# First attention heads: the seventh row block's weights are formed before the eighth's maxima, and a modulation sum moves from the sixth to the fourth row block

## The chip, the cores and the metric

The kernel runs on one core of a Trainium2 chip. The metric is the device time of one execution in microseconds (us). TensorE (PE in the profile, PEld for its weight loads) multiplies, VectorE (DVE) and ScalarE (ACT) do the elementwise work, GpSimd (POOL) splits weights, and SyncE (SP) issues the DMAs.

## What is computed

Two layers of a decoder trunk on x (1024 tokens by 1024 features, float32). Layer 0 has 4 differential attention heads beside 8 dilated sliding-window heads, layer 1 has gated linear attention; each is followed by a SwiGLU feed-forward, and norms and gates are modulated by silu(c) @ ada_w. The change lies in the differential heads:

```python
s = jnp.einsum('bhcqd,bhckd->bhcqk', qb, kf)          # c = 0, 1: two score maps of a head
s = jnp.where(causal, s - slope * dist, -jnp.inf)
p = jax.nn.softmax(s, axis=-1)
w = p[:, :, 0] - lam * p[:, :, 1]                      # the weights of a row block
o = jnp.einsum('bhqk,bhkv->bhqv', w, vf)               # row blocks of 128 queries
mod = jax.nn.silu(c) @ ada_w[l] + ada_b[l]             # the modulation
```

## The kernel before

Each engine has a program of its own, written out by hand; semaphores tie them together, and each engine works strictly in its written order. The heads of layer 0 run as eight blocks b = 0 to 7. Blocks 0 to 3 (kind 0) are the differential heads, one each; 4 to 7 (kind 1) hold two dilated heads each. Within a block, n = 0 to 7 are row blocks of 128 queries; row block n looks at K = 128 (n + 1) keys. In the text row blocks and heads are counted from one: the seventh row block is n = 6.

A row block of kind 0 goes round the engines like this:
- TensorE forms the two score maps (`scores(n)`, L981), two row blocks ahead.
- VectorE, in `biased(b, n)`, adds the bias, takes the row maxima of both maps while writing them from PSUM to `pr[n % 2]` (L2176, two instructions), and negates the maxima (L2181).
- ScalarE exponentiates both maps in place and sums the rows (`exps(n)`, L1572).
- VectorE takes the reciprocals (L2210), forms the coefficient lam * r1 / r0 (L2213, 128x1), and adds the second map times it to the first (L2217). These are the weights; the semaphore `w_done` goes up.
- TensorE waits for `w_done` and transposes the weights (`turn_weights(n)`, L1002) into PSUM banks 4 and 5; ScalarE (L1566) and VectorE (`copies(n)`, L2191) copy them to SBUF, and TensorE multiplies them by the values (`weigh(n)`, L1015), one row block later.

Between these TensorE has other work: for n = 0 to 4 a chunk of the next block's input projection (`chunk`, L824 to L828), for n = 5 to 7 a third of its last chunk (`filler(0)` to `filler(2)`, L846 to L852). Its order for a row block of kind 0 is chunk or filler, `scores(n + 2)`, `turn_weights(n)`, `weigh(n - 1)`. `scores(n)` waits until VectorE has read the maps of row block n - 1. `biased(b, n)` waits for the scores and until the transposes of row block n - 2 have read `pr[n % 2]`.

ScalarE goes through `copies(n - 1)`, `output(n - 2)`, `exps(n + 1)`. After `exps(4)` and `exps(6)` it rounds a streamed weight unit (`hi_u`, L1378), and GpSimd then forms that unit's low part (L702, `w_lo` from `w_raw` and `w_hi`).

VectorE also sums the modulation: `ada_step(e)` (L2139 to L2150) adds one of eight slices of ada_w, scaled by silu(c), to an accumulator (L2143 for the first, L2145 for the others: 128x1024, all operands in SBUF), and then drains. A head has eight such sums, numbered 0 to 7 here, one in each row block before the change. The slices stream through two buffers. SP asks for slice e once sum e - 2 is done, in the order: weight unit, slices 2 to 5, weight unit, slices 6 and 7, weight unit, slices 8 and 9; a weight unit waits for GpSimd to be done with the one two before.

Of the kernel before, what the change touches and what calls it, by code (L numbers as in the profile page):

```python
# [51 lines left out]
def trunk_kernel(nc, xT, cT, weights, ada_w, ada_bT, norm_gT, lam_p, subln_g, w_g2, b_g2, head_g,  # L52
# [5 lines left out]
    with ctx:  # L58
# [47 lines left out]
        def bank(b, n=512):  # L106
            return ps[:, b * 512:b * 512 + n]
# [272 lines left out]
        def lane_count(kind, n, lane):  # L380

            return 1 + sum(g[1] == lane for m in range(n) for g in lanes(kind, m))

        def events(b, t):
            return LANE[0] * min(b, 4) + LANE[1] * max(b - 4, 0) + t
# [1483 lines left out]
        def _(v):  # L1869
# [267 lines left out]
            def ada_step(e):  # L2137

                v.wait_ge(ada_full[e % 2], 16 * (e // 2) + 16)  # L2139
                if e % 8 == 0:  # L2140
                    if e:
                        v.wait_ge(ada_mm, e // 8 + 1)
                    v.tensor_scalar(acc_one, ada_two[:, e % 2, :], cs[:, 0:1], None, ALU.mult).then_inc(ada_used, 1)  # L2143
                else:
                    v.scalar_tensor_tensor(acc_one, ada_two[:, e % 2, :], cs[:, e % 8:e % 8 + 1], acc_one, ALU.mult, ALU.add)\  # L2145
                        .then_inc(ada_used, 1)
                if e % 8 == 7:
                    v.drain().then_inc(acc_done, 1)
                else:
                    v.drain()  # L2150

            def attention():
                def biases(kind):

                    for c in range(kind + 1):
                        v.scalar_tensor_tensor(bias[:, c, :], dist, slope[:, c:c + 1], mask_bias, ALU.mult, ALU.add)
                    v.drain()

                def copy_v(b, group):
                    v.wait_ge(pv_done, 8 * b + 1)  # L2160
                    v.wait_ge(td_done, group)
                    v.tensor_copy(v_tok[:, 4:8, :], bank(5).rearrange("p (m q) -> p m q", q=P)).then_inc(td_free, 1)

                def biased(b, n):

                    kind = b // 4
                    for c in range(2):
                        K = P * (n + 1)
                        col = 2 * n + c
                        v.wait_ge(s_done[c], 8 * b + n + 1)  # L2170

                        if n > 1:
                            v.wait_ge(ta_done, events(b, lane_count(kind, n - 1, 0)))
                            v.wait_ge(td_done, events(b, lane_count(kind, n - 1, 1)))
                        v.sem_inc(waited, 1)
                        v.tensor_tensor_reduce(out=pr[n % 2][:, c, 0:K], in0=ps[:, c * 1024:c * 1024 + K],  # L2176
                                               in1=bias[:, c if kind else 0, 1024 - K:1024], scale=SCORE_SCALE,
                                               scalar=-3.0e38, op0=ALU.add, op1=ALU.max,
                                               accum_out=mx[:, col:col + 1]).then_inc(s_read[c], 1)
                    v.drain()  # L2180
                    v.tensor_scalar(nmx[:, 2 * n:2 * n + 2], mx[:, 2 * n:2 * n + 2], -1.0, None, ALU.mult).then_inc(nm_done, 1)  # L2181

                def block_(kind, b, last=False):
                    before = lambda t: events(b, t)
                    count = 1

                    def copy_d(dst, m):
                        nonlocal count
                        count += 1
                        v.wait_ge(td_done, before(count))  # L2190
                        v.tensor_copy(dst, bank(5)[:, 0:m * P].rearrange("p (m q) -> p m q", q=P)).then_inc(td_free, 1)  # L2191

                    def copies(n):
                        for c, lane, k0, m in lanes(kind, n):
                            if lane == 1:
                                if n > 1:
                                    v.wait_ge(pv_done, 8 * b + n)
                                copy_d(wT[n % 2][c][:, k0:k0 + m, :], m)

                    for n in range(8):  # L2200
                        a0 = 2 * n
                        if n and kind == 1:
                            copies(n - 1)
                        if n < 7:
                            biased(b, n + 1)
                        if n and kind == 0:
                            copies(n - 1)
                        v.wait_ge(exp_done, 16 * b + 2 * n + 2 + 1)
                        if kind == 0:
                            v.reciprocal(r0[:, a0:a0 + 2], rs[:, a0:a0 + 2])  # L2210
                            v.drain()

                            v.scalar_tensor_tensor(coef, r0[:, a0 + 1:a0 + 2], neglam, rs[:, a0:a0 + 1], ALU.mult, ALU.mult)  # L2213
                            v.drain()
                            K = P * (n + 1)
                            p = pr[n % 2]
                            v.scalar_tensor_tensor(p[:, 0, 0:K], p[:, 1, 0:K], coef, p[:, 0, 0:K], ALU.mult, ALU.add)\  # L2217
                                .then_inc(w_done, 1)
                        else:
                            v.reciprocal(r0[:, a0:a0 + 2], rs[:, a0:a0 + 2]).then_inc(w_done, 1)  # L2220
                        if n < 4 and not last:
                            evict(6 * (b + 1) + n)
                        if n == 1 and b:
                            columns(b, b + 1, 1)
                        if b < 7:
                            ada_step(8 * b + n)
                    copies(7)

                    if b == 3:
                        v.wait_ge(tab_full, 48)  # L2230
                        v.memset(slope[:, 0:1], 0.5)
                        v.memset(slope[:, 1:2], 0.25)
                    else:
                        v.tensor_scalar(slope, slope, 0.25, None, ALU.mult)
                    v.drain()
                    if not last:
                        biases((b + 1) // 4)
                        biased(b + 1, 0)
                    if kind == 0:
                        v.wait_ge(sub_root, b + 1)  # L2240
                        v.reciprocal(ms, ms)
                        v.drain()
                        v.tensor_scalar(ms, ms, 1.0 - LAM_INIT, None, ALU.mult)
                        v.drain()
                        v.tensor_tensor(o_sb, o_sb, ms.rearrange("p (n u) -> p n u", u=1).broadcast_to([P, 8, P]), ALU.mult)
                    if kind == 0:
                        v.drain().then_inc(o_ready, 1)
                    if not last:
                        copy_v(b + 1, before(LANE[kind]))
                    for half in range(2):  # L2250
                        v.wait_ge(y_hi, 2 * b + half + 1)
                        high, lower = ((hh[half][:, b, :], hl[half][:, b, :]) if last else
                                       (t[:, half * HALF:(half + 1) * HALF] for t in (y_st_hi, y_st_lo)))
                        if kind == 0:
                            v.scalar_tensor_tensor(lower, bank(4 + half), sub_g, high.bitcast(f32), ALU.mult, ALU.subtract)\
                                .then_inc((ta_free, td_free)[half], 1)
                        else:
                            v.tensor_tensor(lower, bank(4 + half), high.bitcast(f32), ALU.subtract)\
                                .then_inc((ta_free, td_free)[half], 1)
                    v.drain().then_inc(blk_done, 1)  # L2260

                v.wait_ge(tab_full, 32)
                v.memset(slope, 0.25)
                v.drain()
                biases(0)
                copy_v(0, 1)
                biased(0, 0)
                for b in range(HEADS):
                    block_(b // 4, b, b == HEADS - 1)
# [275 lines left out]
```

## Time and profile before

| | us |
|---|---|
| median of three runs | 2646.45 |
| lowest and highest | 2639.69, 2649.98 |
| the profiled execution | 2640.05 |
| its span | 2638.1 |
| TensorE busy | 2517.8 (95%) |
| VectorE busy | 1368.4 (52%) |
| GpSimd busy | 1144.6 (43%) |
| ScalarE busy | 1075.4 (41%) |

The profile is of one execution. In its timeline a line is: start, length, engine, line of the kernel, operation, what is written and read, shapes, and, in brackets, how long the engine had been idle and what released it. The granted clock of TensorE is given as a share of 2.4 GHz, so 0.5 is 1.2 GHz. The four differential heads lie between 95 and 352 us, some 65 us each.

### The profile page before, as it was taken

The numbers are of one execution on the slowest core, as the hardware profiler recorded it, in microseconds if no ns is written. First come the engines' busy times: TensorE is split into PE (matmuls) and PEld (weight loads), VectorE is DVE, ScalarE is ACT, GpSimd is POOL, SyncE is SP. The second block draws the span as 40 slices with busy tenths as digits, with TensorE's granted clock in tenths as the row PEclk, the third lists the DMA queues.
The fourth block names the chain that finished last, engine by engine and source line by source line (L and its number), as shares of the span: only waits on it lengthen the run. The fifth ranks groups of instructions, "written<-read, shape, count | busy, mean of one in ns | idle before, by whom it ended". The sixth has DMA issues, their size and how long they took to land.

```text
span 2638.1 us, 33909 instructions
## 1 busy us (share of the span) xinstructions
PE 2517.8 (95%) x12152; PEld 2058.3 (78%) x12152; DVE 1368.4 (52%) x1877; ACT 1075.4 (41%) x1837; POOL 1144.6 (43%) x648
## 2 busy tenths in 40 slices
PE   5999999999999999999999999998999999999996
PEld 3777778878788888888887777887778888888885
DVE  6566665551574333554356446668556332455145
ACT  3354454344553333334333236555545233334222
POOL 0111111013557777444444434443666777544443
PEclk8999999999999999999999999999999999999998
DMA  6233332234242222442534842213333221343343
GB/s 267 64 104 104 113 112 81 101 116 174 88 128 88 80 71 73 159 135 96 168 111 169 286 136 73 71 67 109 96 100 108 89 88 65 120 143 112 112 136 110
DMA packets 106886, 305.14 MB, mean 116 GB/s; under 512 B 11456, under 2 KB 11776, under 8 KB 106752
## 3 DMA queue, kind: packets, MB, share of 16 engines
q1 hardware_dynamic: 106752, 303.40, 34.1%
q8 instruction: 79, 1.29, 0.2%
q14 instruction: 55, 0.45, 0.1%
HBM read 262.46 MB, written 40.89 MB: 115 GB/s over the span
## 4 chain that ended last, share of the span: by engine, by line
PE 60%; issue 17%; POOL 7%; DVE 7%; DVEq 3%; ACT 3%; POOLq 2%; DMA 1%; SPq 0%; ACTq 0%
PE ps L828 7%; PE ps L824 7%; PE ps L825 7%; PE ps L1277 5%; PE ps L1274 5%; PE ps L1273 5%; POOL w_lo L702 5%; PE ps L1015 3%; PE ps L1304 3%; PE ps L1307 3%; PE ps L1301 3%; PE ps L1105 2%; PE ps L1002 2%; DVEq L2316 2%; PE ps L981 1%
## 5 line engine op out<-in xcount | busy, mean ns | idle before, releaser
L702 POOL TENSOR_TENSOR w_lo<-w_raw,w_hi 128x1024 fp32r<-128x1024 f32 x258 | 629.0, 2441 | 1300.5 <-ACT w_hi L1372 595.9
L824 PE MATMUL ps<-h_hi,w_hi 128*128 128x512 f32 x1200 | 479.3, 399 | 20.8 <-DVE h_lo L1918 9.3
L825 PE MATMUL ps<-h_lo,w_hi 128*128 128x512 f32 x1200 | 469.4, 391 | 0.0
L1372 ACT ACTIVATE w_hi<-w_raw 128x1024 fp32r<-128x1024 f32 x178 | 188.3, 1058 | 436.5 <-PE ps L1307 286.5
L1986 DVE TENSOR_TENSOR a_lo<-arena,a_hi 128x512 fp32r<-128x512 f32 x88 | 205.5, 2336 | 207.7 <-ACT a_hi L1843 207.7
L828 PE MATMUL ps<-h_hi,w_lo 128*128 128x512 f32 x1200 | 298.2, 391 | 0.0
L824 PEld LDWEIGHTS ps<-h_hi,w_hi 128*128 128x128 f32 x1200 | 226.0, 188 | 84.9 <-DVE h_lo L1918 15.6
L828 PEld LDWEIGHTS ps<-h_hi,w_lo 128*128 128x128 f32 x1200 | 226.6, 189 | 47.4
L825 PEld LDWEIGHTS ps<-h_lo,w_hi 128*128 128x128 f32 x1200 | 226.3, 189 | 47.4 <-issue 2.4
L1273 PE MATMUL ps<-comb,w_hi 128*128 128x512 f32 x560 | 217.8, 389 | 0.0
L1274 PE MATMUL ps<-comb,w_hi 128*128 128x512 f32 x560 | 217.8, 389 | 0.0
L751 POOL TENSOR_TENSOR w_lo<-a_f,w_hi 128x512 fp32r<-128x512 f32 x112 | 144.6, 1293 | 79.0 <-ACT w_hi L1466 79.0
L1301 PE MATMUL ps<-a_hi,w_hi 128*128 128x512 f32 x672 | 167.0, 390 | 0.9 <-DVE ybuf L2044 0.9
L1304 PE MATMUL ps<-a_lo,w_hi 128*128 128x512 f32 x672 | 166.0, 389 | 0.0
L1307 PE MATMUL ps<-a_hi,w_lo 128*128 128x512 f32 x672 | 165.9, 389 | 0.0
L1466 ACT ACTIVATE w_hi<-a_f 128x512 fp32r<-128x512 f32 x112 | 70.8, 632 | 230.3 <-PE ps L1277 83.2
L1572 ACT ACTIVATE pr_flat<-pr_flat,small 128x256 f32<-128x256 f32 (+7 forms) x128 | 98.3, 770 | 134.3 <-DVE small L2181 134.2
L1277 PE MATMUL ps<-comb,w_lo 128*128 128x512 f32 x560 | 149.7, 389 | 0.0
L1301 PEld LDWEIGHTS ps<-a_hi,w_hi 128*128 128x128 f32 x672 | 126.0, 188 | 28.5 <-DVE ybuf L2044 1.7
L1307 PEld LDWEIGHTS ps<-a_hi,w_lo 128*128 128x128 f32 x672 | 126.2, 188 | 26.2
L1304 PEld LDWEIGHTS ps<-a_lo,w_hi 128*128 128x128 f32 x672 | 126.2, 188 | 26.2
L1274 PEld LDWEIGHTS ps<-comb,w_hi 128*128 128x128 f32 x560 | 105.1, 188 | 21.8
(269 smaller groups left out, 4374.5 us busy)
## 6 DMA issues: line engine op xcount, KB each, us to landing
w_raw<-weights SPq DMA_DIRECT2D x286, 512.0 KB, 3.6
arena<-ada_w SPq DMA_DIRECT2D x80, 512.0 KB, 3.5
arena<-act_d SPq DMA_DIRECT2D x72, 256.0 KB, 3.8
act_d<-ybuf SPq DMA_DIRECT2D x56, 256.0 KB, 2.2
arena<-ada_w SPq DMA_DIRECT2D x8, 1024.0 KB, 15.1
x<-xT SPq DMA_DIRECT2D x4, 2048.0 KB, 10.9
glr<-weights SPq DMA_DIRECT2D x14, 512.0 KB, 3.6
rinv<-weights SPq DMA_DIRECT2D x28, 256.0 KB, 4.1
```

The source lines that it names most:

```text
L702: pool.tensor_tensor(w_lo[:, s, :], w_raw[:, s, :], w_hi[:, s, :].bitcast(f32), ALU.subtract).then_inc(lo_done, 1)
L824: pe.matmul(bank(b), w, high[:, k, :], start=k == 0, stop=False)
L825: pe.matmul(bank(b), w, low[:, k, :], start=False, stop=False)
L828: mm = pe.matmul(bank(b), w_lo[:, s, k * P:(k + 1) * P], high[:, k, :], start=False, stop=k == KB - 1)
L1273: pe.matmul(bank(b), w, high[:, k, :], start=k == 0, stop=False)
L1274: pe.matmul(bank(b), w, low[:, k, :], start=False, stop=False)
L1277: mm = pe.matmul(bank(b), combo_part(w_lo, q)[:, k * P:(k + 1) * P], high[:, k, :], start=False, stop=k == KB // 2 - 1)
L1301: pe.matmul(bank(m), w_hi[:, slot, cols[m]], a_hi[:, s, :], start=first, stop=False)
L1304: pe.matmul(bank(m), w_hi[:, slot, cols[m]], a_lo[:, s, :], start=False, stop=False)
L1307: mm = pe.matmul(bank(m), w_lo[:, slot, cols[m]], a_hi[:, s, :], start=False, stop=False)
L1372: a.activation(w_hi[:, slot, :], w_raw[:, slot, :], ACT.Copy).then_inc(hi_done, 1)
L1986: v.tensor_tensor(a_lo[:, u % 2, :], act_source(half, u), a_hi[:, u % 2, :].bitcast(f32), ALU.subtract)\
```

## The change

In blocks of kind 0 two things are moved in VectorE's program; no instruction is added or taken away, and no other engine's program is touched.

- `biased(b, 7)`, which stood ahead of the seventh row block's copies and weights, stands behind its weights (L2217).
- The sums are spread otherwise: row blocks n = 0 to 7 do sums 0; 1; 2; 3 and 4; 5; none; 6; 7. Before, row block n did sum n.

Blocks of kind 1 keep their order.

```diff
-                        if n < 7:
+                        if n < 6 or n == 6 and kind:
                             biased(b, n + 1)
                         if n and kind == 0:
                             copies(n - 1)
...
                             v.scalar_tensor_tensor(p[:, 0, 0:K], p[:, 1, 0:K], coef, p[:, 0, 0:K], ALU.mult, ALU.add)\
                                 .then_inc(w_done, 1)
+                            if n == 6:
+                                biased(b, 7)
...
                         if b < 7:
-                            ada_step(8 * b + n)
+                            first, end = ((0, 1), (1, 2), (2, 3), (3, 5), (5, 6), (6, 6), (6, 7), (7, 8))[n] if kind == 0 else (n, n + 1)
+                            for e in range(first, end):
+                                ada_step(8 * b + e)
```

## Rows read from the trace of the kernel before

**Rows 1.** The page's own lines: span, TensorE's share, and the sums' DMA issues.
```profile
span 2638.1 us, 33909 instructions
...
PE 2517.8 (95%) x12152; PEld 2058.3 (78%) x12152; DVE 1368.4 (52%) x1877; ACT 1075.4 (41%) x1837; POOL 1144.6 (43%) x648
...
arena<-ada_w SPq DMA_DIRECT2D x80, 512.0 KB, 3.5
```

**Rows 2.** The waits, 90 to 345 us: waiter, releaser, total us, times, longest.
```profile
PE ps L1002 <- DVE pr_flat L2217: 9.7, 6, 2.3
```

**Rows 3.** Timeline (start, length, engine, line), second head, fifth row block's stretch.
```profile
193.06 0.33 SPq L484 DMA_DIRECT2D arena<-ada_w  x1
193.37 0.96 DVE L2176 CUSTOM_DVE_ANT_0 pr_flat<-ps,arena 128x768 f32<-128x768 f32 x1 [0.34 <-issue]
196.54 0.88 DVE L2217 SCALAR_TENSOR_TENSOR pr_flat<-pr_flat,small 128x640 f32<-128x640 f32 x1
197.34 1.28 DVE L2145 SCALAR_TENSOR_TENSOR rinv<-arena,cs,rinv 128x1024 f32<-128x1024 f32 x1
198.56 0.53 PEld L1002 LDWEIGHTS ps<-ident,pr_flat 128*128 128x128 f32 x5 [0.26 <-issue]
199.61 1.09 DVE L2176 CUSTOM_DVE_ANT_0 pr_flat<-ps,arena 128x896 f32<-128x896 f32 x1 [0.99 <-PE ps L1002]
```

**Rows 4.** Timeline, two neighbouring sums of the later input projection (x2 is both).
```profile
1523.28 2.66 DVE L2077 SCALAR_TENSOR_TENSOR arena<-arena,cs 128x1024 f32<-128x1024 f32 x2
```

**Rows 5.** Timeline, second head: the seventh block's maxima, its exponentials, GpSimd's instruction.
```profile
201.82 0.17 DVE L2181 TENSOR_SCALAR small<-small 128x2 f32<-128x2 f32 x1
202.02 1.04 ACT L1572 ACTIVATE pr_flat<-pr_flat,small 128x896 f32<-128x896 f32 x1 [1.05 <-DVE small L2181]
202.65 1.02 DVE L2217 SCALAR_TENSOR_TENSOR pr_flat<-pr_flat,small 128x768 f32<-128x768 f32 x1
203.73 0.87 PE L1002 MATMUL ps<-ident,pr_flat 128*128 128x128 f32 x6
205.21 2.40 POOL L702 TENSOR_TENSOR w_lo<-w_raw,w_hi 128x1024 fp32r<-128x1024 f32 x1 [13.26 <-ACT w_hi L1378]
205.21 1.23 DVE L2176 CUSTOM_DVE_ANT_0 pr_flat<-ps,arena 128x1024 f32<-128x1024 f32 x1 [0.34 <-issue]
```

**Rows 6.** Timeline, second head: from the eighth maxima to the eighth transposition.
```profile
207.68 0.17 DVE L2181 TENSOR_SCALAR small<-small 128x2 f32<-128x2 f32 x1
207.78 0.42 DVE L2191 COPY wt_flat<-ps 128x256 f32<-128x256 f32 x1
207.88 1.15 ACT L1572 ACTIVATE pr_flat<-pr_flat,small 128x1024 f32<-128x1024 f32 x1 [1.41 <-DVE small L2181]
208.65 1.15 DVE L2217 SCALAR_TENSOR_TENSOR pr_flat<-pr_flat,small 128x896 f32<-128x896 f32 x1
209.03 1.13 ACT L1572 ACTIVATE pr_flat<-pr_flat,small 128x1024 f32<-128x1024 f32 x1
209.86 1.75 PE L1002 MATMUL ps<-ident,pr_flat 128*128 128x128 f32 x7 [2.29 <-DVE pr_flat L2217]
212.19 0.16 DVE L2210 RECIPROCAL small<-small 128x2 f32<-128x2 f32 x1
212.71 1.28 DVE L2217 SCALAR_TENSOR_TENSOR pr_flat<-pr_flat,small 128x1024 f32<-128x1024 f32 x1
215.47 1.04 PE L1002 MATMUL ps<-ident,pr_flat 128*128 128x128 f32 x8
```

**Rows 7.** Timeline, second head, fourth row block: GpSimd beside a modulation sum.
```profile
189.58 2.37 POOL L702 TENSOR_TENSOR w_lo<-w_raw,w_hi 128x1024 fp32r<-128x1024 f32 x1 [31.66 <-ACT w_hi L1378]
190.62 2.41 DVE L2145 SCALAR_TENSOR_TENSOR rinv<-arena,cs,rinv 128x1024 f32<-128x1024 f32 x1
```

**Rows 8.** Windows, second and fourth head: length, engines' busy, clock, DMA.
```profile
209.86:215.47 5.61, 5.61 (x28) 5.22 (x29) 4.46 (x6) 2.63 (x7) 0.00 (x0) 0.70 0.45 136
340.37:344.38 4.01, 4.01 (x28) 3.62 (x28) 3.70 (x6) 2.63 (x7) 0.00 (x0) 1.00 0.52 177
```

## The prediction

> **What bounds the kernel now.** I read the page first, for the whole: TensorE is busy for 95% of the span [rows 1], so time comes off only where TensorE stands still, or where it runs at the lower clock. The change touches heads 1 to 4 of layer 0 alone (kind 0), which lie between 95 and 350 us. So the second view is the list of waits of that stretch: TensorE's matmul side waits 9.7 us for the attention weights of L2217, in 6 waits, the longest 2.3 us [rows 2]. Then I went through the timeline of the second head, instruction by instruction; the other three run alike to a few hundredths up to the transposition of the seventh row block. There TensorE stands for 2.29 us until the seventh weights end at 208.65 + 1.15 = 209.80 [rows 6]. Those weights come late because VectorE has first done a modulation sum and the eighth block's two maxima, from 205.21 on [rows 5]. The last view is the table of windows. From the seventh to the eighth transposition the second head takes 5.61 us at a granted clock of 0.70, the fourth 4.01 us at 1.00 [rows 8]; the first and third look like the second. So in three heads the stand of 2.29 us is followed by a spell at 1.2 GHz instead of 2.4 GHz, worth 5.61 - 4.01 = 1.60 us.
>
> What ends the leg from the seventh to the eighth transposition is TensorE's own queue: in the second head the eighth weights end at 212.71 + 1.28 = 213.99 and are taken up at 215.47 [rows 6]. The slow spell gives VectorE that margin of 1.48 us; the fourth head, at full clock, has little of it, though no wait stands before its eighth transposition either.
>
> **Part 1: the sum moved to the fourth row block.** Sum 4 now follows sum 3, and 5 comes in the fifth block, none in the sixth. Two neighbouring sums take 2.66 us, one 1.28 [rows 4, 3], so VectorE reaches the sixth block's maxima 1.38 us later than at 193.37. Its fifth weights end at 196.54 + 0.88 + 1.38 = 198.80 instead of 197.42. TensorE wanted them at 198.56, where it waited for nothing but issue [rows 3]; with 0.06 us for the hand-over (209.80 to 209.86 [rows 6]) it starts at 198.86, 0.30 late. VectorE's sum 5 ends at 197.34 + 1.38 + 1.28 = 200.00, and after the 0.34 us of issue that stands before such maxima [rows 3] the seventh maxima begin at 200.34. They began at 199.61, after 0.99 us of waiting for TensorE [rows 3]. That wait absorbs half; 0.73 us of delay is left, and it goes on to TensorE at the sixth transposition, which already waits for VectorE. The sum's DMA does not bind: buffer 5 is asked for at 193.06 [rows 3] and 3.5 us [rows 1] bring it to 196.6, before 198.7. On SP the sixth and seventh buffers are asked for earlier than now, the weight load between them waits for GpSimd as before. Cost of part 1: +0.73 us a head.
>
> **Part 2: the swap in the seventh row block.** Count from the start of the seventh maxima's negation, 201.82 [rows 5]. TensorE's sixth transposition ends at 203.73 + 0.87 = 204.60, so 2.78; VectorE's copy can follow 0.10 later, at 2.88. From such a copy to the end of the seventh weights it is 209.80 - 207.78 = 2.02 us [rows 6], of which the weights are the last 1.15. Undisturbed they would end at 4.90, and TensorE, through with its filler at 209.86 - 2.29 - 201.82 = 5.75, would find them ready.
>
> They are not undisturbed. GpSimd's instruction of L702 starts at 205.21, which is 3.39, and lasts 2.40, to 5.79 [rows 5]. It hangs on ScalarE, which has done the seventh exponentials by then, not on VectorE's order, so it stays at 3.39. Today it lies beside the maxima, which read PSUM and take 1.23 us beside it [rows 5]. A sum of L2145, an instruction of the same kind as the weights (two operands of SBUF), took 2.41 us instead of 1.28 beside L702: it ended at 193.03, 1.08 after L702's end at 191.95 [rows 7, 3]. So such an instruction makes 1.28 - 1.08 = 0.20 us of headway and then stands until GpSimd is done. The weights, due at 3.75, would end at 5.79 + 1.15 - 0.20 = 6.74 at the earliest. The tiny L2213 ahead of them is due at 3.45, 0.06 after GpSimd's start, and is of the same kind; if it is held as well, add its 0.30: 7.04. I take 7.04, because the two times are that close and both are fixed by the same rows.
> The Trainium skill ("SBUF — State Buffer", section "Who interferes with whom") says that a VectorE instruction with two SBUF inputs and a GpSimd instruction that reads SBUF exclude each other, and that whichever issues first keeps the port for its whole length. On the first half this trace agrees (2.41 against 1.28 us); the second half is a rival below.
>
> TensorE then begins the seventh transposition at 7.10 and stands for 7.10 - 5.75 = 1.35 us instead of 2.29. But now the eighth maxima come behind these weights. They start 0.08 before the weights' end (as sum 4 does in [rows 3]), at 6.96; the exponentials follow 207.88 - 205.21 = 2.67 later, last to 210.16, so 2.28 us, then 0.06 hand-over, 0.52 from the reciprocal to the weights, 1.28 for these, 0.06 to TensorE [rows 5, 6]: 6.96 + 2.67 + 2.28 + 0.06 + 0.52 + 1.28 + 0.06 = 13.83. Sum 6 and the copy fit in the 2.3 us of the exponentials. TensorE would be free at 7.10 + 4.01 = 11.11. So a stand of 2.72 us arises before the eighth transposition, where there is none now.
>
> With part 1's 0.73 the eighth transposition starts at 14.56. Today it starts at 215.47 - 201.82 = 13.65 in heads 1 to 3, and at 8.04 + 4.01 = 12.05 in the fourth. Loss: 3 x 0.91 + 2.51 = 5.2 us.
>
> **The clock.** These 13.65 already hold the slow spell of 1.60 us. The new stand of 2.72 us is longer than the one that is followed by the spell in three heads of four; the one of 1.35 is shorter. What follows the eighth transposition (the seventh and eighth products, the next head's first scores) is on the path. I take three spells again: 3 x 1.60 = 4.8. None would be 0, four 6.4.
>
> Sum: 5.2 + 4.8 = +10.0 us. No later stage gets it back or adds to it: what follows is chained to TensorE.
>
> **Rivals.**
> A, the same order, but the clock does not fall behind the new stand: +5.2. For it: the fourth head had 2.28 us of stand and kept 1.00.
> B, the weights get ahead of GpSimd and L702 waits for them; nobody needs its result before the next head. Then they end at 4.90, TensorE never stands before block seven, and the eighth transposition comes at 4.82 + 6.87 + 0.73 = 12.42: three heads gain 1.23, the fourth loses 0.37, together -3.3; with spells behind the 1.9 us stand that is left, up to +3. Against it: the weights are due 0.36 us after GpSimd's start. The page of the skill named above states the rule for who waits, first come first served; no row here shows VectorE first.
> C, slower. The spell at 1.2 GHz lasts longer, since two stands of 1.35 and 2.72 us follow one another within 7 us. Now it costs 1.6 a head; at twice the length 3.2 in all four heads make 12.8 + 5.2 = +18.0. It decides from (13.2 - 5.2) / 4 = 2.0 us a head on.
> D, faster. The stand before block seven goes and none comes before block eight: 4 x 2.29 + 3 x 1.60 = -14.0. Against it: the eighth maxima have nowhere else to go.
> E, the change does not do what it says, since the seventh weights wait for something else: 0. The exponentials are done at 210.16 - 207.68 = 2.5 after the negation at block eight and sooner at block seven, so this is unlikely.
>
> **How the numbers follow.** Chances: forecast 0.54, A 0.15, B 0.17, C 0.09, D 0.02, E 0.03. The profiled execution has 2640.05 us (span 2638.1 [rows 1]), which is 6.4 below the median of the three runs, 2646.45 (2639.69 to 2649.98). Against its own time the sum gives 2650.05; against the median 2656.45. Since four executions lie within 10.3 us, I set it on the mean of all four, 2644.05: 2654 us. Low end: B on that mean, 2640.7, hence 2640. High end: C, 2662, and two for the spread of the runs: 2664. About 0.5%, 13.2 us, is what a measurement of this kernel can tell from no change. Faster takes D and a measurement gone astray with B: 0.03. Slower takes C and 0.06 for the upper end of the forecast (four spells give 11.6): 0.15. The same: 0.82.
>
> **What would show it.** Right: L2217 of the seventh block (128x896) is about 2 us long instead of 1.15, or starts only after L702's end; TensorE's wait before seven transpositions falls to about 1.35 and one of about 2.7 appears before the eight; seventh to eighth transposition takes 6.7 us in all four heads; the seventh maxima start without waiting for TensorE. Wrong: L2217 at 1.15 us with GpSimd's instruction late (B); a granted clock of 1.00 behind the new stand (A); under 0.5 for longer than now (C).

## The result, and the profile after

The changed kernel takes 2653.34 us (median of 10 runs, 2648.46 to 2658.4), the kernel before 2643.98 (10 runs, 2639.69 to 2650.07). The ratio is 1.0038, with a 95% interval of 1.0027 to 1.0049: 10.0 us slower (7.1 to 13.0), and inside the 0.5% that was called no change; the two medians lie 9.4 us apart. All ratios are over every execution but one of e1 that took 10011.71 us.

The page of the changed kernel: 9.8 us more of span, and hardly more work on TensorE.

```profile
span 2647.9 us, 33909 instructions
...
PE 2521.2 (95%) x12152; PEld 2060.0 (78%) x12152; DVE 1378.4 (52%) x1877; ACT 1074.3 (41%) x1837; POOL 1142.8 (43%) x648
```

The list of waits from 90 to 350 us, TensorE's matmul side: 9.7 us in [rows 2] have become 15.7, and 6 waits 17. The fourth head's stand of 2.65 us, at 351.15, lies behind this window.

```profile
PE ps L1002 <- DVE pr_flat L2217: 15.7, 17, 2.7
```

The second head's timeline (start, length, engine, line), fifth row block to the seventh maxima, against [rows 3]. The fifth transposition (L1002, x5) now waits for VectorE, and the seventh maxima (L2176) follow VectorE's own sum with 0.34 us of issue, and no longer TensorE.

```profile
199.22 1.28 DVE L2145 SCALAR_TENSOR_TENSOR rinv<-arena,cs,rinv 128x1024 f32<-128x1024 f32 x1
199.36 0.77 PE L1002 MATMUL ps<-ident,pr_flat 128*128 128x128 f32 x5 [0.27 <-DVE pr_flat L2217]
200.84 1.09 DVE L2176 CUSTOM_DVE_ANT_0 pr_flat<-ps,arena 128x896 f32<-128x896 f32 x1 [0.34 <-issue]
```

The swap's place, against [rows 5] and [rows 6], from the seventh maxima's negation at 203.04 on. L2213, which works on one column, takes 2.33 us: it started 0.08 after GpSimd's L702 and ended 0.02 after it. Only then come the seventh weights (L2217), and 0.08 before their end the eighth maxima.

```profile
203.04 0.17 DVE L2181 TENSOR_SCALAR small<-small 128x2 f32<-128x2 f32 x1
203.88 1.02 DVE L2217 SCALAR_TENSOR_TENSOR pr_flat<-pr_flat,small 128x768 f32<-128x768 f32 x1
206.43 2.39 POOL L702 TENSOR_TENSOR w_lo<-w_raw,w_hi 128x1024 fp32r<-128x1024 f32 x1 [13.99 <-ACT w_hi L1378]
206.51 2.33 DVE L2213 SCALAR_TENSOR_TENSOR small<-small 128x1 f32<-128x1 f32 x1
208.91 1.15 DVE L2217 SCALAR_TENSOR_TENSOR pr_flat<-pr_flat,small 128x896 f32<-128x896 f32 x1
209.98 1.22 DVE L2176 CUSTOM_DVE_ANT_0 pr_flat<-ps,arena 128x1024 f32<-128x1024 f32 x1
210.12 0.98 PE L1002 MATMUL ps<-ident,pr_flat 128*128 128x128 f32 x7 [1.32 <-DVE pr_flat L2217]
```

What follows from these maxima: exponentials, reciprocal, the eighth weights, and TensorE, which has stood for 2.66 us.

```profile
212.65 1.16 ACT L1572 ACTIVATE pr_flat<-pr_flat,small 128x1024 f32<-128x1024 f32 x1 [4.95 <-DVE small L2181]
215.05 0.17 DVE L2210 RECIPROCAL small<-small 128x2 f32<-128x2 f32 x1 [0.54 <-ACT pr_flat L1572]
215.59 1.28 DVE L2217 SCALAR_TENSOR_TENSOR pr_flat<-pr_flat,small 128x1024 f32<-128x1024 f32 x1
216.93 1.17 PE L1002 MATMUL ps<-ident,pr_flat 128*128 128x128 f32 x8 [2.66 <-DVE pr_flat L2217]
```

Windows of the same head (length, busy time by engine, granted clock), from the seventh to the eighth transposition, against [rows 8], and from the eighth on. The clock is at 2.4 GHz in the first, and spends most of the second at 1.2.

```profile
210.12:216.93 6.81, 4.15 (x28) 3.48 (x28) 5.87 (x11) 4.18 (x9) 0.00 (x0) 1.00 0.41 143
216.93:221.60 4.67, 4.67 (x28) 4.36 (x28) 3.19 (x4) 1.34 (x5) 0.00 (x0) 0.63 0.36 116
```

### The profile page after: what moved, and what is told of

Read it like the earlier page. It is cut to its first block, busy times and chain, and to the rows that moved or that the text cites. A ratio compares the mean times of both kernels' runs of the same rounds, so it can differ in the third digit from the quotient of the medians.

```text
span 2647.9 us, 33909 instructions
## 1 busy us (share of the span) xinstructions
PE 2521.2 (95%) x12152; PEld 2060.0 (78%) x12152; DVE 1378.4 (52%) x1877; ACT 1074.3 (41%) x1837; POOL 1142.8 (43%) x648
## 4 chain that ended last, share of the span: by engine, by line
PE 57%; issue 17%; DVE 8%; POOL 7%; DVEq 3%; ACT 3%; POOLq 2%; DMA 1%; ACTq 1%; SPq 1%
PE ps L828 7%; PE ps L824 7%; PE ps L825 7%; PE ps L1274 5%; PE ps L1277 5%; PE ps L1273 5%; POOL w_lo L702 5%; PE ps L1015 3%; PE ps L1304 3%; PE ps L1307 3%; PE ps L1301 3%; PE ps L1105 2%; PE ps L1002 2%; DVEq L2320 1%; POOL w_lo L751 1%
## 5 line engine op out<-in xcount | busy, mean ns | idle before, releaser
L702 POOL TENSOR_TENSOR w_lo<-w_raw,w_hi 128x1024 fp32r<-128x1024 f32 x258 | 627.2, 2434 | 1311.5 <-ACT w_hi L1372 592.7
L1301 PE MATMUL ps<-a_hi,w_hi 128*128 128x512 f32 x672 | 167.0, 390 | 0.5 <-DVE ybuf L2044 0.3
L1301 PEld LDWEIGHTS ps<-a_hi,w_hi 128*128 128x128 f32 x672 | 126.0, 188 | 28.1 <-DVE ybuf L2044 1.2
```

What stands on the lines that cost most here:

```text
L702: pool.tensor_tensor(w_lo[:, s, :], w_raw[:, s, :], w_hi[:, s, :].bitcast(f32), ALU.subtract).then_inc(lo_done, 1)
L1301: pe.matmul(bank(m), w_hi[:, slot, cols[m]], a_hi[:, s, :], start=first, stop=False)
```

## Experiments

A measure that is finer than whole runs is used beside them: the stretch from the first weights of the first head to the start of the fourth head's final copy (L1634), from each kernel's profiled execution, with the number of slow spells in the four heads. A spell is a stretch at a granted clock of 0.5; each of them in the four heads lasted 3.4 us. "The eighth" is the start of the eighth transposition, counted as in the prediction from the negation of the seventh maxima. "Clock" is the granted clock over a whole execution, averaged over all executions of the kernel; that of the kernel before, run beside them, was 0.9870 for e1 to e4, 0.9868 for e4b to e7 and 0.9869 for e8 and e9 (0.9869 over all 79).

| kernel | seventh weights end | the eighth | stretch, us | spells | clock | ratio to before (95%) |
|---|---|---|---|---|---|---|
| before | 7.98 | 13.65 (fourth head 12.05) | 256.12 | 3 | 0.9869 | 1 |
| changed | 7.02 | 13.89 | 264.98 | 2 | 0.9869 | 1.0038 (1.0027 to 1.0049) |
| e1 sum alone | 7.73 | 11.79 (third 13.43) | 255.04 | 1 | 0.9877 | 1.0005 (0.9994 to 1.0016) |
| e2 swap alone | 7.02 | 13.89 | 261.98 | 1 | 0.9868 | 1.0038 (1.0025 to 1.0051) |
| e3 L702 late | 4.91 | 11.77 | 254.95 | 0 | 0.9887 | 0.9997 (0.9989 to 1.0006) |
| e4 16 products | 7.03 | 14.66 | 264.74 | 0 | 0.9890 | 1.0038 (1.0024 to 1.0051) |
| e4b 10 products | 7.03 | 13.89 | 262.33 | 0 | 0.9886 | 1.0017 (1.0004 to 1.0030) |
| e5 sums, L702 early | 7.66 | 11.73 (second 13.32) | 251.69 | 1 | 0.9868 | 1.0000 (0.9986 to 1.0015) |
| e6 the same, swap | 4.90 | 11.77 | 258.43 | 4 | 0.9870 | 0.9992 (0.9980 to 1.0004) |
| e7 and split | 4.90 | 11.09 | 247.78 | 0 | 0.9884 | 0.9970 (0.9957 to 0.9983) |
| e8 e7, no swap | 8.13 | 12.2 to 13.85 | 256.36 | 3 | 0.9864 | 1.0000 (0.9988 to 1.0013) |
| e9 e7 again | 4.91 | 11.10 | 247.82 | 0 | 0.9891 | 0.9967 (0.9956 to 0.9978) |

The stretches of e2 and e6 begin inside one more spell (95.2 to 98.8 us and 96.8 to 100.4), which is not counted here; it makes the way from the first weights to the first head's negation 39.67 and 39.81 us long, 1.3 and 1.4 more than without it.

### e1: the sum's move alone

```diff
-                        if n < 6 or n == 6 and kind:
+                        if n < 7:
                             biased(b, n + 1)
...
-                            if n == 6:
-                                biased(b, 7)
```
(against the changed kernel)

> Part 1 alone: the sums in the new places, the eighth maxima still ahead of the seventh weights. Times count from the start of the seventh maxima's negation. My theory: 0.73 us of delay a head up to there. The eighth maxima then start at 2.9 instead of 3.4, but their small negation (all in SBUF) would fall beside GpSimd's L702 (3.4 to 5.8) and is held until 5.8, so the seventh weights end at 7.9, about as before (7.98), and the four heads lose 0.65 us each: +2.6 us against the kernel before, spells of 1.2 GHz as before. Rival: the negation is not held; the weights end at 7.45 and the loss is 0.2 us a head, +0.8. Rival: the moved sum costs nothing at all, and the heads gain 0.5 each: -2.

Measured: 1.0005, +1.3 us (-1.6 to +4.2). The second head's timeline: the eighth maxima start 3.07 after the negation (202.79 here), and their own negation (L2181) is indeed held, but for 0.10 us only, since it came due 0.25 us before GpSimd's end (208.33, against 206.18 + 2.40).

```profile
205.86 1.23 DVE L2176 CUSTOM_DVE_ANT_0 pr_flat<-ps,arena 128x1024 f32<-128x1024 f32 x1 [1.21 <-PE ps L1002]
206.18 2.40 POOL L702 TENSOR_TENSOR w_lo<-w_raw,w_hi 128x1024 fp32r<-128x1024 f32 x1 [13.99 <-ACT w_hi L1378]
208.33 0.27 DVE L2181 TENSOR_SCALAR small<-small 128x2 f32<-128x2 f32 x1
209.37 1.15 DVE L2217 SCALAR_TENSOR_TENSOR pr_flat<-pr_flat,small 128x896 f32<-128x896 f32 x1
210.58 0.53 PEld L1002 LDWEIGHTS ps<-ident,pr_flat 128*128 128x128 f32 x5 [2.46 <-DVE pr_flat L2217]
```

The weights end at 7.73, between the two sizes given. The head gains 0.25 there, loses 0.7 before, and the profiled execution has fewer spells than before; the sum's move is close to neutral. The expectation's mechanism held, but the weights end 0.2 earlier than it had them, and the interval is too wide to tell its +2.6 us from a rival's +0.8.

### e2: the swap alone

```diff
-                            first, end = ((0, 1), (1, 2), (2, 3), (3, 5), (5, 6), (6, 6), (6, 7), (7, 8))[n] if kind == 0 else (n, n + 1)
-                            for e in range(first, end):
-                                ada_step(8 * b + e)
+                            ada_step(8 * b + n)
```
(against the changed kernel)

> Part 2 alone: the eighth maxima behind the seventh weights, sum n in row block n as before. Theory: the sum in the sixth row block ends at 3.05, so the copy and L2213 still come before GpSimd's L702 is through; L2213 is held to 5.8, the seventh weights end at 7.04 as in the changed kernel, TensorE stands 1.3 us before block seven and 2.7 before block eight. The eighth transposition starts at 13.8: +0.2 in three heads and +1.8 in the fourth, +2.3 us, and with one spell at 1.2 GHz (1.6 us) in two to four heads +5.5 to +8.7 against before, 1 to 4 less than the changed kernel. Rival: without the 0.73 us of part 1 nothing is lost (0), the swap is harmless and the moved sum is the cause.

Measured: 1.0038, +10.0 us (6.6 to 13.5), above the 5.5 to 8.7 expected, and not the 1 to 4 us below the changed kernel that were expected either; only the stretch shows these (3.0). So the swap carries the loss, and the rival that blamed the moved sum falls. Second head: the sum (L2145) now stands ahead of L2213, which comes due later, is still caught, and ends with GpSimd's instruction; the weights end at the same 7.02. The reciprocal before it (L2210) also starts beside L702 and is not held.

```profile
204.90 1.28 DVE L2145 SCALAR_TENSOR_TENSOR rinv<-arena,cs,rinv 128x1024 f32<-128x1024 f32 x1
206.52 2.40 POOL L702 TENSOR_TENSOR w_lo<-w_raw,w_hi 128x1024 fp32r<-128x1024 f32 x1 [13.26 <-ACT w_hi L1378]
206.68 0.15 DVE L2210 RECIPROCAL small<-small 128x2 f32<-128x2 f32 x1
206.91 2.02 DVE L2213 SCALAR_TENSOR_TENSOR small<-small 128x1 f32<-128x1 f32 x1
209.00 1.15 DVE L2217 SCALAR_TENSOR_TENSOR pr_flat<-pr_flat,small 128x896 f32<-128x896 f32 x1
```

From negation to negation the heads take 65.57, 66.67 and 65.90 us, against 66.28, 67.58 and 66.64 in the changed kernel (the same spell stands in the second leg of both): part 1 costs 0.71 to 0.91 a head, of 0.73 forecast.

### e3: GpSimd's instruction out of the way

```diff
-                        if n == 5 and b < 6:
+                        if n == (7 if kind == 0 else 5) and b < 6:
                             hi_u(3 * b + 6)
```
(ScalarE's program, against the changed kernel)

> The changed kernel, with ScalarE's rounding of the next weight unit, and so GpSimd's L702, two row blocks later in the differential heads (behind the eighth exponentials). Theory (GpSimd holds L2213 and the weights): L2213 takes 0.22 us again, the seventh weights end at 4.9, TensorE does not wait before block seven, waits 1.9 us before block eight, which starts at 11.7 plus 0.73: against before -3.3 us without slow spells, up to +3 with four; 5 to 8 us faster than the changed kernel. If VectorE is first, GpSimd is the one that waits: L702 would be due some 12 us after the negation, while sum 7 runs, and would start or end late. Rival (the weights are late for another reason, VectorE's own queue or the exponentials): L2213 is short but the weights still end near 7, time as the changed kernel, +9.

Measured: 0.9997, -0.8 us (-2.9 to +1.6), some 11 us less than the changed kernel. First head, negation at 137.33: L2213 takes 0.22 again, the weights end at 4.91, TensorE does not wait before block seven and waits 2.08 before block eight. And where VectorE is first, GpSimd waits: L702 starts during sum 7 (148.97 to 150.25) and takes 2.96 us instead of 2.40.

```profile
140.79 0.22 DVE L2213 SCALAR_TENSOR_TENSOR small<-small 128x1 f32<-128x1 f32 x1
141.09 1.15 DVE L2217 SCALAR_TENSOR_TENSOR pr_flat<-pr_flat,small 128x896 f32<-128x896 f32 x1
148.97 1.28 DVE L2145 SCALAR_TENSOR_TENSOR rinv<-arena,cs,rinv 128x1024 f32<-128x1024 f32 x1
149.11 1.09 PE L1002 MATMUL ps<-ident,pr_flat 128*128 128x128 f32 x8 [2.08 <-DVE pr_flat L2217]
149.50 2.96 POOL L702 TENSOR_TENSOR w_lo<-w_raw,w_hi 128x1024 fp32r<-128x1024 f32 x1 [23.18 <-ACT w_hi L1378]
```

The gain of 3.3 was not reached. L702 of the following unit now meets the next head's first negation and holds it for 2.19 us; the head's end, from the eighth transposition to L1634, takes 10.21 us instead of 9.81. With 0.75 of part 1 and 1.90 gained at the eighth that is -0.75 in the first head.

```profile
154.51 2.35 POOL L702 TENSOR_TENSOR w_lo<-w_raw,w_hi 128x1024 fp32r<-128x1024 f32 x1 [2.05 <-ACT w_hi L1378]
154.70 2.19 DVE L2181 TENSOR_SCALAR small<-small 128x2 f32<-128x2 f32 x1
```

### e4 and e4b: work put into TensorE's stand

```diff
                     if kind == 0:
+                        if n == 7:
+                            pe.wait_ge(s_read[0], 8 * b + 9)
+                            pe.wait_ge(s_read[1], 8 * b + 9)
+                            for i in range(16):
+                                pe.matmul(bank(0, P), ident[:, :], ident[:, :], start=True, stop=True)
                         turn_weights(n)
```
(against the changed kernel; e4b has `range(10)`)

> The changed kernel with 16 products of 128x128 on TensorE, 2.0 us of work that nobody reads, put into its stand before the eighth transposition of each differential head (they write a bank of scores already read). Theory (the slow spells come from the stand): the stand falls to 0.7 us, the granted clock stays 1.00 in all four heads, and the eighth transposition does not come later; against the changed kernel 3.2 us less (its two spells of 1.6), against before about +6. Rival (the spells have nothing to do with this stand): the spells stay and the time is that of the changed kernel, +9 to +10. Rival: the added work itself delays block eight: above +10.

Measured: 1.0038, +10.0 us (6.3 to 13.5), near the third case, and not the +6 of the theory. A product is two matmuls; 32 of them took 3.73 us, more than the stand, so that the eighth transposition came at 14.66. No spell was left in the four heads all the same.

```profile
216.48 3.73 PE L1055 MATMUL ps<-ident 128*128 128x128 f32 x32
220.05 1.04 PE L1002 MATMUL ps<-ident,pr_flat 128*128 128x128 f32 x8
```

> As the first kernel with added products, but 10 instead of 16, since 16 took 3.7 us (two matmuls each, 0.116 us apiece) and overfilled the stand of 2.65 us. Ten take 2.3 us and leave some 0.4 us of stand before the eighth transposition. Theory (the slow spells of the differential heads come from that stand): no spell in the four heads, the eighth transposition at 13.9 us after the negation as in the changed kernel; from the first weights to the end of the fourth head about 261.8 us (the changed kernel has 265.0 with two spells). Rival: the spells stay, 265.

Measured: 1.0017, +4.5 us (1.1 to 7.9). Again no spell in the four heads, the eighth at 13.89, and a stretch of 262.33 us (261.8 expected): 2.65 less than the changed kernel with its two spells. This is TensorE's side of e4b in the second head; 0.41 us of stand is left.

```profile
214.55 2.39 PE L1055 MATMUL ps<-ident 128*128 128x128 f32 x20
217.35 1.09 PE L1002 MATMUL ps<-ident,pr_flat 128*128 128x128 f32 x8 [0.41 <-DVE pr_flat L2222]
```

### e5 and e6: sums and GpSimd early, without and with the swap

```diff
+                        if kind == 0 and n < 2:
+                            ada_step(8 * b + 2 * n)
                         if n < 4 and not last:
                             evict(6 * (b + 1) + n)
...
-                            ada_step(8 * b + n)
+                            first, end = ((1, 2), (3, 4), (4, 5), (5, 6), (6, 6), (6, 6), (6, 7), (7, 8))[n] if kind == 0 else (n, n + 1)
+                            for e in range(first, end):
+                                ada_step(8 * b + e)
...
-                        if n == 5 and b < 6:
+                        if n == (4 if kind == 0 else 5) and b < 6:
                             hi_u(3 * b + 6)
```
(against the kernel before; e6 adds the change's swap)

> The order of maxima and weights of the kernel before. Two things moved in the differential heads: the sums run early, 0 and 2 ahead of the evictions of the first two row blocks, where VectorE waits anyway, then 1, 3, 4, 5 and none in the fifth and sixth row block; and ScalarE's rounding of the next unit, so GpSimd's L702, comes before the seventh maxima instead of beside the swap's place. Theory: no 0.73 us of delay, the eighth maxima start at 3.1 us after the negation, nothing is held, the seventh weights end at 7.6 and the eighth transposition starts at 11.7 with a stand of 1.9 us before block seven: 2.0 us less in each of the three heads with spells and 0.4 in the fourth, -6.3 us, up to 3 given back by spells. Rival: the early sums delay the first row blocks, and nothing is gained.

Measured: 1.0000 (-3.7 to +4.0 us), a miss as a time, though the timeline is as expected: 7.66 and 11.73, 1.97 us of stand, and a stretch 4.4 us shorter. The profiled execution (span 2632.7 us) is the fastest of the twelve, 2634.69 to 2651.49. Over all twelve the granted clock is 0.9868, as before, so the two spells fewer of this one trace are not what the twelve show. Without the spells the eighth comes 0.32 us a head earlier than before (11.73 against 12.05), 1.3 us in all, which the interval can't tell from nothing: most of the 2.0 us a head that were expected was a spell of 1.6 counted as gone. TensorE's lines of the second head, the one with the spell (5.60 us between the two transpositions), show the stand before the seventh and no wait before the eighth.

```profile
207.13 0.98 PE L1002 MATMUL ps<-ident,pr_flat 128*128 128x128 f32 x7 [1.96 <-DVE pr_flat L2217]
212.73 1.03 PE L1002 MATMUL ps<-ident,pr_flat 128*128 128x128 f32 x8
```

> As the kernel with early sums and early GpSimd, but with the change's swap: the seventh weights ahead of the eighth maxima. This asks what the swap is worth once neither the sum nor GpSimd stands in its way. Theory: the weights end at 4.9 and TensorE finds them ready, but the eighth maxima, exponentials and weights follow one another from there, and the eighth transposition starts at 11.8 with 2.0 us of stand before it: the stand has moved, -6 us against before, the same as without the swap within 1 us. Rival: the swap is worth its 1.9 us a head once the way is free: -13.

Measured: 0.9992, -2.1 us (-5.3 to +1.1): no 6 us gained, and far from the rival's 13. As in e5, the six counted three spells as gone. The seventh weights end at 4.90, no wait is left before block seven, and behind the 2.08 us of stand before block eight there is a spell in each head of the profiled execution. The second head's eighth transposition, and the window from it on, at a clock of 0.58:

```profile
215.95 1.58 PE L1002 MATMUL ps<-ident,pr_flat 128*128 128x128 f32 x8 [2.08 <-DVE pr_flat L2217]
```

```profile
215.93:220.00 4.07, 4.05 (x22) 4.06 (x22) 3.21 (x4) 0.89 (x2) 0.00 (x0) 0.58 0.40 129
```

VectorE's sum 6 (211.53) is through before the exponentials are, and the reciprocal waits 0.54 us for ScalarE, so here the sum delays nothing:

```profile
211.53 1.28 DVE L2145 SCALAR_TENSOR_TENSOR rinv<-arena,cs,rinv 128x1024 f32<-128x1024 f32 x1
214.07 0.17 DVE L2210 RECIPROCAL small<-small 128x2 f32<-128x2 f32 x1 [0.54 <-ACT pr_flat L1572]
```

With nothing in the way of either order, the swap is worth nothing: the eighth comes at 11.77 with it and 11.73 without it.

### e7 and e9: the maxima of block eight negated map by map

```diff
-                    v.drain()
-                    v.tensor_scalar(nmx[:, 2 * n:2 * n + 2], mx[:, 2 * n:2 * n + 2], -1.0, None, ALU.mult).then_inc(nm_done, 1)
+                        if n == 7 and kind == 0:
+                            v.drain()
+                            v.tensor_scalar(nmx[:, col:col + 1], mx[:, col:col + 1], -1.0, None, ALU.mult)\
+                                .then_inc((nm_first, nm_done)[c], 1)
+                    if n < 7 or kind:
+                        v.drain()
+                        v.tensor_scalar(nmx[:, 2 * n:2 * n + 2], mx[:, 2 * n:2 * n + 2], -1.0, None, ALU.mult).then_inc(nm_done, 1)
...
-                            a.wait_ge(nm_done, 8 * b + n + 1)
+                            if b < 4 and n == 7 and c == 0:
+                                a.wait_ge(nm_first, b + 1)
+                            else:
+                                a.wait_ge(nm_done, 8 * b + n + 1)
```
(on e6; sum 6 moves to the fifth row block)

> As the kernel before this one (swap, early sums, early GpSimd), with the eighth row block's maxima negated map by map, so that ScalarE starts on the first map's exponentials while VectorE is still at the second map's maxima; the seventh sum (6) goes to the fifth row block. Theory: what bounds now is the chain maxima, exponentials, weights of block eight; overlapping the two maps takes 0.9 us off it, the eighth transposition starts at 10.9 and TensorE stands 1.1 us before it: 3.5 us less a head than with the swap alone in three heads, -9 to -10 us against before. Rival: TensorE is bounded elsewhere by then, and the time is that of the kernel without the split, -6.

Measured: 0.9970, -7.9 us (-11.4 to -4.5), faster than both kernels, though less than the 9 to 10 expected. Sum 6 moved as well, but in e6 it delayed nothing, so the gain at the eighth (11.77 to 11.09) is the split's. Second head: the first exponentials (L1576) start with the second map's maxima (L2180) instead of after them, and the eighth comes at 11.09 with 1.40 us of stand and no spell in any head.

```profile
203.51 1.21 DVE L2180 CUSTOM_DVE_ANT_0 pr_flat<-ps,arena 128x1024 f32<-128x1024 f32 x1
205.01 1.15 ACT L1576 ACTIVATE pr_flat<-pr_flat,small 128x1024 f32<-128x1024 f32 x1 [1.67 <-DVE small L2186]
205.11 1.23 DVE L2180 CUSTOM_DVE_ANT_0 pr_flat<-ps,arena 128x1024 f32<-128x1024 f32 x1
206.63 1.15 ACT L1576 ACTIVATE pr_flat<-pr_flat,small 128x1024 f32<-128x1024 f32 x1 [0.37 <-DVE small L2186]
208.43 1.28 DVE L2226 SCALAR_TENSOR_TENSOR pr_flat<-pr_flat,small 128x1024 f32<-128x1024 f32 x1
209.77 1.09 PE L1003 MATMUL ps<-ident,pr_flat 128*128 128x128 f32 x8 [1.40 <-DVE pr_flat L2226]
```

> The kernel with the split negation once more, word for word, on the same chip as the one without the swap, so that the two can be set side by side: -8 us against before, as it was.

Measured: 0.9967, -8.7 us (-11.6 to -5.8).

### e8: the same without the swap

```diff
-                        if n < 6 or n == 6 and kind:
+                        if n < 7:
                             biased(b, n + 1)
...
-                            if n == 6:
-                                biased(b, 7)
```
(against e9)

> The fastest kernel so far (swap, early sums, early GpSimd, maxima of block eight negated map by map) with the swap undone: the eighth maxima ahead of the seventh weights again. Theory (the swap pays only where the chain behind it is short enough): the eighth maxima start at 3.1 us after the negation, the seventh weights end at 7.9 and TensorE stands 2.2 us before block seven; the eighth block is ready when TensorE is, at 7.9 + 4.0 = 11.9. With the swap that is 11.09, so the swap is worth 0.8 us a head here, 3.3 us in all, plus what spells the longer stand brings: -5 or less against before. Rival: the order makes no difference here either, -8.

Measured on the same chip as e9: 1.0000 (-3.2 to +3.4 us), where -5 or less was expected. The weights end at 8.13 (7.9 expected), TensorE stands 2.43 us before block seven (second head), and a spell follows in three heads. Here the swap is worth 2642.53 - 2633.87 = 8.7 us; the stretches say 256.36 - 247.82 = 8.5. Net of spells (12.2 in the first head, against 11.10) it is 1.1 us a head, 4.4 in all; the rest is the clock, which over all executions is 0.9864 in e8 and 0.9891 in e9.

```profile
208.51 1.15 DVE L2226 SCALAR_TENSOR_TENSOR pr_flat<-pr_flat,small 128x896 f32<-128x896 f32 x1
209.71 1.38 PE L1003 MATMUL ps<-ident,pr_flat 128*128 128x128 f32 x7 [2.43 <-DVE pr_flat L2226]
```

## Why the prediction was right

It gave 2654 us, +10.0 on the mean of four executions; measured were 2653.34 and +10.0. By its steps:

- **Part 1.** Right. The fifth transposition starts late behind VectorE, the wait of 0.99 us before the seventh maxima is used up, and the delay that is left is 0.74 us in the first head (39.14 against 38.40 us from first weights to negation), 0.73 forecast.
- **GpSimd's hold on the swap's place.** Right to the instruction: L2213 was due just behind L702, and it is this tiny instruction, not L2217, that stands for 2.33 us. Weights to 7.02 (7.04 forecast), a stand of 1.32 (1.35). Of the two signs named, the first (L2217 about 2 us long) did not come, the second (it starts only after L702's end) did. e3 shows the cause by taking L702 away: 4.91.
- **The new stand.** Right: 2.66 us before the eighth transposition (2.72 forecast), which comes at 13.89 (13.83), 6.81 us after the seventh. With part 1 the eighth is late by 0.96 to 1.07 us in three heads and 2.58 in the fourth, together 5.6 (5.2 forecast).
- **The clock.** The mechanism is borne out, the count in the profiled execution was not: two spells in the four heads, the second and the fourth, where three were taken. Head by head the stretch grew by 1.01, 2.51, 1.16 and 4.18 us: with a spell 1.6 more. e4b takes the stand away, and both spells go; it is 5.5 us faster than the changed kernel, at a clock of 0.9886 against 0.9869. In the twelve profiled executions a spell follows in 15 of the 32 heads that have a stand of 1.96 us or more, and in none of the 16 whose longest is 1.40 us or less (e4, e4b, e7, e9). Of the 9.8 us of span 8.9 lie in the heads; the rest is the net of what comes later, with spells that only one of the two traces has, among them one of the changed kernel at 597 to 600 us in a dilated head that the change does not touch and that had none before. That this one trace comes so near to 10.0 is luck.
- **Rivals.** B needed the weights ahead of GpSimd; they were behind it by 0.08 us. Its rule was right (e3), its price was not: -3.3 were forecast for it, and -0.8 came, as GpSimd's next instruction falls on the next head's first negation (0.40 us a head). A came true in two heads of the profiled execution and not in the other two; over all executions the clock did not change, which speaks against it. C: the spells are as long as they were, some 3.4 us. D never had its condition; even e6, where the weights are ready at 4.90, only moved the stand. E: the weights waited for what was said.

**The totals from two terms.** The prediction's sum, 3 x 0.91 + 2.51 + 3 x 1.60, is also 4 x 2.51: four times the loss of a head at full clock, with as many spells as before. The runs bear out this reading. An estimate made after the results: take four times the eighth less the 12.05 us of the fourth head before, with 0.74 added where part 1 is in (and 0.40 more in e3, for the head's end); then add the fall of the clock against the kernel before times 2642 us, the time of that kernel, since at a clock of 0.5 half the time is lost (from unrounded clocks).

| kernel | four heads at full clock, us | clock, us | both, us | measured, us (95%) |
|---|---|---|---|---|
| changed | 10.3 | 0.0 | 10.3 | 10.0 (7.1 to 13.0) |
| e1 | 1.9 | -1.7 | 0.2 | 1.3 (-1.6 to 4.2) |
| e2 | 7.4 | 0.8 | 8.1 | 10.0 (6.6 to 13.5) |
| e3 | 3.4 | -4.5 | -1.0 | -0.8 (-2.9 to 1.6) |
| e4 | 13.4 | -5.2 | 8.2 | 10.0 (6.3 to 13.5) |
| e4b | 10.3 | -4.8 | 5.5 | 4.5 (1.1 to 7.9) |
| e5 | -1.3 | 0.0 | -1.3 | 0.0 (-3.7 to 4.0) |
| e6 | -1.1 | -0.6 | -1.8 | -2.1 (-5.3 to 1.1) |
| e7 | -3.8 | -4.3 | -8.2 | -7.9 (-11.4 to -4.5) |
| e8 | 0.6 | 1.3 | 1.9 | 0.0 (-3.2 to 3.4) |
| e9 | -3.8 | -5.8 | -9.6 | -8.7 (-11.6 to -5.8) |

All eleven estimates lie in the measured intervals. The changed kernel loses 2.6 us a head and keeps its clock; where TensorE no longer stands 2 us (e4, e4b, e7, e9), the clock rises as well. e3 is the exception: it stands 2.08 us and its clock rises too.

What is open: why a stand of 2.08 us is followed by a spell in none of the heads of e3 and in all four of e6. One execution of each is profiled, and the length of a stand alone doesn't tell; e3's clock over all executions (0.9887 against 0.9870 in e6) says that its executions spend less time at the lower clock. Single traces also differ outside the heads. That of e2 is 11.7 us longer in its span than that of the kernel before, with 5.9 in the heads; the other 5.8 come in one place, where TensorE's L1301 has waited 3.61 us at 2298.75 (0.49 in the kernel before) and the clock is at 0.5 from 2297 to 2304. Whether that recurs in other executions isn't known.

## What to carry to other kernels

Moving a consumer's input forward pays only as far as the work it overtakes can wait. Here both halves, the seventh weights and the eighth maxima, feed TensorE within 6 us of each other, so the stand went from one to the other; the swap paid (e8 against e9) once the second chain had been shortened by letting ScalarE start map by map. Before counting a vanished spell as gain, compare the clock over many executions, since the executions of one kernel differ (0.984 to 0.989 in e5). Before moving a VectorE instruction with two SBUF operands, look at what GpSimd does in the new place, and look at the smallest instructions too: one column can stand for 2.3 us.

## What the runs showed of the hardware

The hold is first come, first served, in both directions: VectorE's L2213 started 0.08 us behind GpSimd and took 2.33 us instead of 0.22, and GpSimd's L702, started 0.53 us behind a sum, took 2.96 instead of 2.40. It catches one instruction with a single operand as well: the negation L2181 (128x2, in SBUF) took 2.19 us in e3, against 0.17. It doesn't catch all of that kind: the reciprocal L2210 (128x2, in SBUF) took 0.15 us beside L702 in e2, as it does elsewhere. The maxima and copies that read PSUM ran at their own pace beside L702 (1.23 us in [rows 5]). The Trainium skill ("SBUF — State Buffer", section "Who interferes with whom") states the rule, first to issue keeps the port, and the case of `tensor_scalar`; these runs agree.
